# Two modulation pairs moved into the expert router, one pair out of the projections

## The reference

```python
ada_x = split(silu(c) @ w_ada + b_ada, 6)         # shift, scale, gate, for mixer and ffn
x = x + ada_x[2] * token_mixer(modulate(rmsnorm(x), ada_x[0], ada_x[1]), ...)
h = modulate(rmsnorm(x), ada_x[3], ada_x[4])
aff = softmax(h @ w_router); gate, idx = top_k(aff.T, 32)      # 16 experts
ye = (silu(h[idx] @ w1[e]) * (h[idx] @ w3[e])) @ w2[e] * gate   # w1, w3: 1024x2048, w2: 2048x1024
x = x + ada_x[5] * scatter_add(ye)
x = rmsnorm(x, final_norm_g)
for l in range(2):                                 # second block, its own vector c_2
    ada = silu(c_2) @ w_ada_2[l] + b_ada_2[l]      # 6144 columns per layer
    x = x + g_m * attention_mixer(...)             # uses ada of its layer
    x = x + g_f * ffn(...)
```

## Time and profile before

| | |
|---|---|
| runs (3) | 2438.51 us median, 2428.66 to 2440.57 |
| profiled execution | 2437.47 us, its span 2435.1 us |
| TensorE busy | 2037.1 us (84%), mean granted clock 0.916 |
| VectorE, ScalarE busy | 411.6 us (17%), 328.4 us (13%) |
| DMA | 648.48 MB, mean 266 GB/s |
| expert tiles into the ring | 186 issues of 2048 KB, median 16.3 us to landing |
| chain that ended last | PE 63%, DMA 32%, DVE 3%, ACT 1% |

### The profile page before, as it was taken

The page is one execution under the profiler, slowest core; times in us unless marked ns, Lnnn a source line. Parts: engine busy times, 40 slices in busy tenths (PEclk is TensorE's granted clock), DMA queues, the critical chain, the costliest instruction groups (busy, mean ns, idle before and its releaser), DMA issues.

```text
span 2435.1 us, 28156 instructions
## 1 busy us (share of the span) xinstructions
PE 2037.1 (84%) x12190; PEld 1313.4 (54%) x12190; DVE 411.6 (17%) x1137; ACT 328.4 (13%) x739; POOL 0.2 (0%) x4
## 2 busy tenths in 40 slices
PE   7999998766666666666656799999999999899999
PEld 4468787421111112111111347778888658788888
DVE  4113242200000000000000214431000124411000
ACT  4132120200000000000000112421000122501000
POOL 0000000000000000000000000000000000000000
PEclk9999999878888888888887899899999999899999
DMA  9157577499999999999999945116334535045341
GB/s 357 47 191 270 198 253 302 199 428 429 428 429 428 429 428 429 428 428 428 428 428 428 407 177 176 66 70 242 139 137 156 198 132 208 1 173 208 135 177 35
DMA packets 147872, 648.48 MB, mean 266 GB/s; under 512 B 10645, under 2 KB 17410, under 8 KB 123016
## 3 DMA queue, kind: packets, MB, share of 16 engines
q1 hardware_dynamic: 141254, 643.16, 66.7%
q10 hardware_dynamic: 6530, 4.01, 0.6%
HBM read 646.10 MB, written 1.05 MB: 266 GB/s over the span
## 4 chain that ended last, share of the span: by engine, by line
PE 63%; DMA 32%; DVE 3%; ACT 1%; issue 1%; ACTq 0%; SPq 0%; DVEq 0%; PEldq 0%
DMA ring<-in_w_exp 31%; PE bank L822 27%; PE bank L836 6%; PE bank L2284 6%; PE bank L1617 4%; PE bank L1381 4%; PE bank L1632 2%; PE bank L592 1%; PE bank L855 1%; PE bank L700 1%; PE bank L453 1%; DMA ring<-in_w_branch_ml 1%; PE bank L2083 1%; PE bank L2090 1%; PE bank L1305 1%
## 5 line engine op out<-in xcount | busy, mean ns | idle before, releaser
L822 PE MATMUL bank<-hx,ring 128*128 128x256 f32 (+1 forms) x2944 | 656.1, 385 | 0.7 <-ACT hx L718 0.7
L822 PEld LDWEIGHTS bank<-hx,ring 128*128 128x128 f32 x2944 | 560.2, 191 | 94.2 <-issue 19.6
L1617 PE MATMUL bank<-ring,arena 128*32 128x512 f32 x1968 | 303.1, 750 | 209.0 <-DMA ring<-in_w_exp 198.7
L1617 PEld LDWEIGHTS bank<-ring,arena 128*32 128x32 f32 x1968 | 60.4, 123 | 433.3 <-DMA ring<-in_w_exp 314.0
L1632 PE MATMUL bank<-ring,arena 128*32 128x512 f32 x1008 | 161.0, 780 | 79.3 <-DMA ring<-in_w_exp 68.4
L836 PE MATMUL bank<-ring,hx 128*128 128x512 f32 (+1 forms) x384 | 152.9, 560 | 1.1 <-ACT hx L778 0.7
L2284 PE MATMUL bank<-arena,ring 128*128 128x256 f32 x704 | 152.4, 379 | 1.5 <-DVE arena L2317 1.5
L2284 PEld LDWEIGHTS bank<-arena,ring 128*128 128x128 f32 x704 | 133.6, 190 | 20.0 <-issue 1.9
L1632 PEld LDWEIGHTS bank<-ring,arena 128*32 128x32 f32 x1008 | 32.8, 132 | 190.0 <-DMA ring<-in_w_exp 108.0
L836 PEld LDWEIGHTS bank<-ring,hx 128*128 128x128 f32 x384 | 72.8, 190 | 80.1 <-issue 76.2
L1675 DVE COPY arena<-bank 128x256 f32<-128x256 f32 x16 | 6.8, 425 | 526.9 <-PE bank L1622 526.9
(11 more groups left out here) (372 smaller groups left out, 1555.4 us busy)
## 6 DMA issues: line engine op xcount, KB each, us to landing
ring<-in_w_exp SPq DMA_DIRECT2D x186, 2048.0 KB, 16.3
ring<-in_w_ada SPq DMA_DIRECT2D x36, 2048.0 KB, 12.2
ring<-in_w_in SPq DMA_DIRECT2D x29, 2048.0 KB, 9.0
ring<-in_w_ffn_in SPq DMA_DIRECT2D x20, 2048.0 KB, 7.9
ring<-in_w_ffn_out SPq DMA_DIRECT2D x10, 2048.0 KB, 8.1
ring<-in_w_out SPq DMA_DIRECT2D x6, 2048.0 KB, 12.1
arena<-in_w_exp SPq DMA_DIRECT2D x4, 2048.0 KB, 16.2
ring<-in_w_up_nsa SPq DMA_DIRECT2D x2, 2048.0 KB, 8.9
```

The costliest lines, as they stand in the source:

```text
L822: ins = pe.matmul(b[:, o:o + n], w[:, k, j * P:(j + 1) * P], h[:, k, :], start=k == 0, stop=k == KD - 1)
L1617: ins = pe.matmul(banks[s][32 * j:32 * j + 32, :], e_xe[:, 2 * t + kk, :], w[:, kk, 512 * j:512 * j + 512], start=t + kk == 0, stop=t + kk ...
```

## The change

- The stream has eight pairs of "later" tiles instead of ten. The pair after the projection hy1 is gone, so the pairs behind it each move one place on; after num3 there is one pair instead of two.
- The last two pairs (tiles 16 to 19) become "late" pairs with the numbers -2 and -1, at the end of `stream`, behind the output weights. They use the "late" functions. TensorE does pair -2 ahead of the logits and pair -1 while VectorE searches.
- In the router the affinity transposes now stand ahead of the four clearing matmuls.
- The bank claims of the experts are made where they are needed, and the waits in `act_later` and `dve_later` calls move with the groups.
- SP issues the four late tiles between the expert tiles: two after "full merge07", two after extra tile 4. Tiles 7 and 8 of expert 0 now come after extra tile 9.

```diff
     for t in range(3):
-        (tiles_and_ada if t < 2 else tiles)(f"hy{t}", wide(w_in, 512 * t, 512 * t + 512))
+        (tiles_and_ada if t < 1 else tiles)(f"hy{t}", wide(w_in, 512 * t, 512 * t + 512))
...
-    for t in range(2):
-        tiles_and_ada("", [])
+    tiles_and_ada("", [])
...
     tiles("out1_", wide(A["w_out"][0], 0, D))
+    tiles("late-2_", later[16:18])
+    tiles("late-1_", later[18:20])
...
-        if g >= 2:
-            act.wait_ge(*at(f"full late cols{g - 2}"))
+        act.wait_ge(*at(f"full late cols{g - 2}" if g >= 0 else "full later cols3"))
...
+        dst = adaX[2][:, 8 * g:8 * g + 8] if g >= 0 else adaX[1][:, 48 + 8 * g:56 + 8 * g]
+        v.tensor_tensor(dst, c[:, 2, :], C2[:, 48 + 8 * g:56 + 8 * g], ALU.add).then_inc(
...
@@ pe_project
         pe_linear_T(pe, "hy1_", "hy10", x, N)
-        pe_later(pe)
         pe_context(pe)
@@ pe_branches
         pe_mlstm_num(pe, 3)
         pe_later(pe)
-        pe_later(pe)
-        pe_later_turn(pe, 4)
+        pe_later_turn(pe, 3)
@@ act_branches
         act_merge_gates(act, 0)
+        act_later(act, 1)
         act_merge_gates(act, 1)
-        act_later(act, 2)
...
         act_mlstm_head(act, 2)
+        act_later(act, 2)
         act_merge_gates(act, 3)
         act_mlstm_head(act, 3)
-        act_later(act, 3)
         act_second_loads(act)
...
         act.activation(w4[:, 0:8], w4[:, 0:8], ACT.Sqrt).then_inc(*AC.step("mlstm root"))
-        act_later(act, 4)
+        act_later(act, 3)
@@ pe_route
         turn["n"] = 4
+        pe_late(pe, -2)
...
         tokens(1, 1)
+        pe.wait_ge(*at("affinity"))
+        b = bank(pe, "affT")
+        for c in range(NC):
+            ins = pe.transpose(b[0:EXPERTS, c * P:(c + 1) * P], e_aff[:, c, :], ident[:, :])
+        ins.then_inc(*PE.step("full affT"))
         pe.wait_ge(*at("y zero"))
...
-        pe.wait_ge(*at("affinity"))
-        b = bank(pe, "affT")
-        for c in range(NC):
-            ins = pe.transpose(b[0:EXPERTS, c * P:(c + 1) * P], e_aff[:, c, :], ident[:, :])
-        ins.then_inc(*PE.step("full affT"))
+        pe_late_turn(pe, -2)
+        pe_late(pe, -1)
         pe.wait_ge(*at("slots"))
...
+        pe_late_turn(pe, -1)
         pe.wait_ge(*at("h tokens"))
@@ sync
-        for n in range(N_PRE):
+        for n in range(N_PRE - 4):
             one(n, stream[n])
...
         sp.wait_ge(*at("full merge07"))
+        one(N_PRE - 4, stream[N_PRE - 4])
+        one(N_PRE - 3, stream[N_PRE - 3])
         extra_tile(2)
         extra_tile(3)
         sp.wait_ge(*at("merged0 done7"))
         extra_tile(4)
-        for t in (5, 6, 7, 8):
+        one(N_PRE - 2, stream[N_PRE - 2])
+        one(N_PRE - 1, stream[N_PRE - 1])
+        for t in (5, 6):
             sp.wait_ge(*at(f"used {ring_of[t] - RING}"))
             expert_tile(ring_of[t], 0, t)
         sp.wait_ge(*at("h ffn0 done"))
         extra_tile(9)
+        for t in (7, 8):
+            sp.wait_ge(*at(f"used {ring_of[t] - RING}"))
+            expert_tile(ring_of[t], 0, t)
```

More of the change, by code:

```diff
@@ L575, in program @@
     LATER = ([("adaX0b", 16 + 16 * g, both[:1], c_bada) for g in range(2)]
-             + [("ada20", 16 * g, [(2, adaX[1])], C2[:, 0:48]) for g in range(3)])
+             + [("ada20", 16 * g, [(2, adaX[1])], C2[:, 0:48]) for g in range(2)])
     next_later = [0]
@@ L659, in dve_late @@
         c = bank_of(f"late cols{g}")[:, 0:256].rearrange("p (q m) -> p m q", m=32)
-        v.tensor_tensor(adaX[2][:, 8 * g:8 * g + 8], c[:, 2, :], C2[:, 48 + 8 * g:56 + 8 * g], ALU.add).then_inc(
-            *DV.step(f"free late cols{g}", f"ada21 part{g}"))
+        dst = adaX[2][:, 8 * g:8 * g + 8] if g >= 0 else adaX[1][:, 48 + 8 * g:56 + 8 * g]
+        v.tensor_tensor(dst, c[:, 2, :], C2[:, 48 + 8 * g:56 + 8 * g], ALU.add).then_inc(
+            *DV.step(f"free late cols{g}", f"ada21 part{g}" if g >= 0 else "ada20"))
     def mark_used(pe, key):
@@ L1015, in act_project @@
                                            bias=c_bo[:, 2 * i + j:2 * i + j + 1]).then_inc(*AC.step(f"free o{i}", "o ready"))
-        act_later(act, 1)
         act_hy_turn(act, 1)
@@ L1250, in dve_mlstm @@
                 dve_mlstm_out(v, h - 1)
-            if h == 1:
+            if h == 3:
                 dve_later(v, 2)
@@ L1362, in dve_hyena @@
                 v.tensor_tensor(zc[:, c, :], b[:, :], hyt[:, c, (o + 1) * HY:(o + 2) * HY], ALU.mult).then_inc(*DV.step(f"free idft{o}{c}", f"z{o + 1}"))
-            if o == 0:
+            if o:
                 dve_later(v, 1)
-                DV.stage("hyena")
     merged = view(hx, KD * N, P, KD, N)
@@ L1482, in pe_route @@
                                    skip_group_check=True).then_inc(*PE.step("full " + key))
-        pe.wait_ge(*at("affinity"))
-        b = bank(pe, "affT")
-        for c in range(NC):
-            ins = pe.transpose(b[0:EXPERTS, c * P:(c + 1) * P], e_aff[:, c, :], ident[:, :])
-        ins.then_inc(*PE.step("full affT"))
+        pe_late_turn(pe, -2)
+        pe_late(pe, -1)
+        PE.stage("route")
         pe.wait_ge(*at("slots"))
@@ L1492, in pe_route @@
         ins.then_inc(*PE.step("full postok"))
-        for b in range(4):
-            claim(pe, b, f"expert bank{b}")
+        pe_late_turn(pe, -1)
         pe.wait_ge(*at("h tokens"))
         pe.wait_ge(*at("first slots"))
+        claim(pe, 2, "expert bank2")
         pe_gather(pe, "first ")
@@ L1499, in pe_route @@
         pe_gather_turn(pe, "first ")
+        for b in (0, 1, 3):
+            claim(pe, b, f"expert bank{b}")
     def pe_gather(pe, name):
@@ L1515, in act_route @@
     def act_route(act):
+        act_late(act, -2)
         AC.stage("route")
@@ L1528, in act_route @@
                 act.copy(e_htok[:, c, 512 * i:512 * i + 512], b[:, :]).then_inc(*AC.step(f"free htok{c}{i}", "h tokens"))
+        act_late(act, -1)
+        AC.stage("route")
         act.wait_ge(*at("first gathered"))
@@ L1571, in dve_route @@
             *DV.step("first slots"))
+        dve_late(v, -2)
+        dve_late(v, -1)
+        DV.stage("route")
         v.wait_ge(*at("first turned"))
@@ L2456, in _ @@
         dve_rope(v)
-        dve_later(v, 4)
         m_out[0][1](v)
```

## The result

The changed kernel takes 2417.99 us in the median of its runs (2415.25 to 2421.15, one of 10916 us apart), the kernel before 2434.76 (2425.03 to 2440.57). The ratio is 0.9933 [0.9917, 0.9948], a gain of 16.3 us, with 12.7 to 20.2 as its interval. The ratio leaves the run of 10916 us out. The forecast was a gain of 22.7, and 2416 us.

The account below looks back on a forecast made before the run. The expert-weight stream was taken as the bound, its restart set by TensorE's sixth tile of expert 0. Gains of 16.0 us up to the mixer's start and 6.7 in the router sum to 22.7, giving 2416 us (2412 to 2419).

Parts of the forecast that it names:

- The bound: Expert loop: a weight stream of fixed length, so a microsecond off the path to its restart is one off the whole.
- The pair out of the projections: End of the projections: moving one modulation pair out gains 3.4 us, with bounds of 2.6 and 3.7.
- The mixer's start: End of the branches: mixer starts at 364.3 instead of 380.29, a gain of 16.0 us, bounds 13 and 17.
- rival 2: Before the mixer: branch_ml or the small loads come 2 to 4 us later than taken; gain 19 to 21, chance 0.11.
- The mixer: The mixer's own duration: nothing changes, counted as 0, with 3.1 us as the bound on the good side.
- The router: Mixer's end to TensorE's sixth expert 0 tile: filled waits and a faster clock bring it 6.7 us earlier.
- Rival 1: Router: the clock falls in short waits and gives the gain back; total gain 13 to 16 us, chance 0.15.
- The DMA queue: Expert 0's ring tiles: four ada tiles (19.6 us) go between them, hidden with 6 to 8 us to spare.
- The number: Whole kernel: a gain of 22.7 us gives 2416 us; chance of the forecast 0.58.

Follow-up runs that it names:

- the loads alone on the kernel before: The kernel before with 12 of the second block's 20 small loads issued at the start of the branches; ratio 1.0003, 2431.98 us.
- The first experiment: The changed kernel with 12 of the second block's 20 small loads (all but the gain rows) issued at the start of the branches; ratio 0.9896, 2406.22 us.
- the two pieces: The kernel before with only the affinity transposes ahead of the clearing, or only the gap before the logits filled with useless matmuls; 2427.87 and 2433.21 us.
- the exchange alone: The kernel before with only the affinity transposes put ahead of the clearing matmuls; 2427.87 us, a single time.
- the gain rows last: The changed kernel with 12 small loads issued early and the 8 gain rows loaded after the router's small loads; ratio 0.9895, 2409.18 us.

## Why the prediction was right, and where it was off

- **The bound.** Right. A restart 18.7 us earlier gave experts that end 19.2 earlier, and the ratio says 16.3 (12.7 to 20.2). Over the twelve traces the first ring tile moves by 26.0 us (454.90 to 480.92), and the time of the same execution less that position stays between 1949.8 and 1957.1. Among the medians one seems not to fit: with the loads alone on the kernel before the first ring tile came 3.9 us earlier in the trace and the median did not move. But the traced execution, 2430.40, was the fastest of its ten, so trace and time agree and the step is within the scatter of that kernel's front.
- **The pair out of the projections.** Right: forecast 3.4, measured 4.7, of which 1.2 was there before. The last convolution starts at 224.41 (225 to 226 forecast), its transposes take 2.23 instead of 1.97 us, the 0.3 that was to show, and the wait for ScalarE is 0.72.
- **The mixer's start.** This step failed in its size. The term was 16.0 and measured 9.05. The prediction put the last issue of the small loads at 354.8 and 9.0 us to landing, 363.8; it was 357.58 and 13.3 (13.4 for the last load itself), and TensorE went on at 371.00. I had moved the list of loads with its old duration and its old landing time, though it now ran beside the branch weights, the output weights and two expert tiles (SP issued these six from 343.68 to 363.81), where before only the last ada tiles were under way until 360.42. That is rival 2, with a larger size than the 2 to 4 us it was given. The first experiment shows that it was the small loads, since with 12 of them taken out of that place the mixer starts at 364.84. That the tiles beside them make them slow is supported by the traces with the front of before, where with branch_hy issued 3 us sooner the list took up to 16.4 us and the last load up to 16.6 to land; an experiment that moves the tiles alone was not made. The 10.9 and 9.0 were also the best of a range, taken from one execution, where the last load itself took 10.1. I had also not seen that ScalarE's root and copy stand behind the issues in its list: 3.53 us of waiting on VectorE and 6.37 on TensorE, hidden only because the loads were later still.
- **What the Trainium skill said there** (DMA: Bandwidth & Descriptors, Issuing engines are not separate DMA queues), that transfers from both queues interleave, agrees with the traces: branch_ml took 12.4 us with no small loads beside it and 14.0 to 19.1 with them. I had applied it to the large tile alone, and the small ones paid.
- **The mixer.** 0 was counted, with 3.1 as the bound; 1.4 came. It starts slow in every kernel: its first 128 records take 29.55 us behind a wait of 2.05, 29.33 behind one of 6.50 and up to 30.8 elsewhere, against 27.79 for as many of the output stage.
- **The router.** Forecast 6.7, measured 8.2. Logits 3.61 (3.5 forecast), no wait ahead of the slots, clock 1.00. Two sizes were small: 5.8 instead of 4.9 to the experts' start, and 2.45 instead of 1.8 for the first four tiles, which run at 1.77 each, not at the 1.92 that I took from a tile beside the stream. Rival 1, the clock that takes the gain back, is refuted in the changed kernel. It is real in the kernels with one wait left, where after 2.3 us or more of waiting for the slots the first four tiles take 8.5 to 10.0 us instead of 7.07.
- **The DMA queue.** Right in that no expert tile was waited for. Tile 7, issued at 447.95, landed 12.9 us later at 460.9 and was used at 462.21 + 2 x 1.79 = 465.8. Tile 8, issued at 449.69, landed 16.0 later at 465.7 and was used at 472.05. So 4.9 and 6.3 us were to spare, a little less than the 6 to 8 forecast.
- **The number.** 2416 was counted from a median of 2438.51 of three runs, and the kernel before came to 2434.76 in eleven. So 2417.99 was hit with a gain 6 us smaller than forecast and a starting point 4 us lower. That the time came within 2 us of 2416 is luck to that extent. The 7 us missing at the mixer were partly made up by the mixer and the router.

The fastest version is that with the small loads early, at 0.9896 and 0.9894, about 9 to 10 us below the changed kernel.

## What to carry to other kernels

When a transfer or a list of issues is moved, take its landing time from what runs beside it at the new place, from more than one execution, and look for what stands behind the issues on the engine that makes them. Small loads that don't depend on anything belong well ahead of the work that waits for them: the 12 early ones went out from 231.23 on, beside a DMA share of 1.02 to 1.06, most in 0.45 us each. A wait of TensorE before a stage that matters can cost more than its length, by the slower clock of the next matmuls. In the traces here filling both waits gave more than the sum of the two pieces, and even useless matmuls did it.

## What the runs showed of the hardware

- Issuing small loads isn't of constant price. In ScalarE's list of 20 most took 0.4 to 0.6 us, single ones up to 2.02 in the changed kernel and 3.46 with the exchange alone, and ScalarE's own work behind the list waited 12.31 us. A busy DMA share isn't enough for it: between 351 and 360 us of the kernel before it was 0.96 to 1.09, and no issue took more than 0.72. The slow ones came as SP issued new 2 MB tiles (with the exchange at 357.73, 359.48 and 361.22, the long issues at 358.70 and 361.36). That isn't all of it: with the gain rows last, one load of 0.5 KB took 5.58 us to issue at 370.46, some 9 us after SP's last.
- Eight loads of 32 KB, 0.26 MB in all, lengthened the landing of a 2 MB tile from 12.4 to about 18 us, with four or five of them issued ahead of it. With twenty loads, and these eight all behind it, it was 14.1.
- After 2.28 us idle the gather ran at half rate (1.94 us). After 0.33, 0.49 and 1.02 us in the same place it stayed at 1.07 and the tiles at 7.07. But num3 kept the upper level after 2.53 us (0.49 for its first matmuls), where it had the lower one after 2.96 (0.80). What sets the limit was not tried.
